# Mixer of a two-block network: three tiles on the unnormed input, gate tile later, VectorE's program in another order

## What is computed

```python
hn = rmsnorm(x, norm_mix_g)            # x * rsqrt(mean(x*x) + eps) * g, per token
z = hn @ w_in                          # 1024 -> u,v | a,g | xc | oc | 4+4 gates
# head group A: u * (causal W_s @ standardize(v) + b_s)        "gating"
# group B: 31-tap causal depthwise conv of a*sigmoid(g), group norm, silu   "long convolution"
# group C: 4-tap causal conv + silu of xc ("short convolution"), then 4 mLSTM heads:
#   logi, logf = gates; running sum and running max over the tokens ("rows"); q, k, v;
#   scores * exp(weights); standardize; skip; sigmoid(oc)
h = x + concat([y_a, y_b, y_c]) @ w_out
# then cross attention on mem, a gated MLP and the whole second block
```

## Time and profile before

| what | value |
|---|---|
| median of 3 runs | 1892.98 us (1892.58 to 1893.07) |
| the profiled execution's own time | 1892.58 us |
| its span in the trace | 1890.8 us |
| PE busy with matmuls | 1866.1 us, 99% of the span |
| POOL / DVE / ACT busy | 1078.7 / 780.8 / 429.9 us |
| share of PE in the chain that ended last | 96% |

### The profile page before, as it was taken

One profiled execution on the slowest core, in us unless ns is written; L12 is line 12 of the kernel. 1 busy time (PEld: TensorE's weight loads), 2 busy tenths in 40 slices (PEclk: granted clock), 3 DMA queues, 4 the chain that ended last, 5 costly groups with the idle time before them and its releaser, 6 DMA issues.

```text
span 1890.8 us, 24359 instructions
## 1 busy us (share of the span) xinstructions
PE 1866.1 (99%) x8992; PEld 1509.4 (80%) x8992; DVE 780.8 (41%) x1274; ACT 429.9 (23%) x840; POOL 1078.7 (57%) x622
## 2 busy tenths in 40 slices
...
GB/s 227 110 81 95 104 96 38 90 100 96 116 89 112 101 78 144 89 46 1 78 79 96 92 100 89 89 90 89 105 96 45 78 90 102 101 100 96 100 101 45
DMA packets 47456, 173.78 MB, mean 92 GB/s; under 512 B 5265, under 2 KB 5905, under 8 KB 46737
## 3 DMA queue, kind: packets, MB, share of 16 engines
...
## 4 chain that ended last, share of the span: by engine, by line
PE 96%; DVE 2%; ACT 1%; DMA 0%; issue 0%; SPq 0%; DVEq 0%
PE acc L513 17%; PE acc L515 17%; PE acc L514 17%; PE acc L540 6%; PE acc L537 6%; PE acc L536 6%; PE acc L592 1%; PE acc L990 1%; PE acc L594 1%; PE acc L593 1%; PE misc L1006 1%; PE misc L1026 1%; PE acc L1182 1%; PE acc L1184 1%; PE acc L1183 1%; PE acc L613 1%
## 5 line engine op out<-in xcount | busy, mean ns | idle before, releaser
L2623 POOL TENSOR_SCALAR w_hi<-raw 128x1024 fp32r<-128x1024 f32 x309 | 335.1, 1084 | 759.3 <-PE acc L540 280.5
L2625 POOL TENSOR_TENSOR w_lo<-raw,w_hi 128x1024 fp32r<-128x1024 f32 x309 | 748.3, 2422 | 25.8
L513 PE MATMUL acc<-x_hi,w_hi 128*128 128x512 f32 x872 | 340.1, 390 | 0.0
L515 PE MATMUL acc<-x_hi,w_lo 128*128 128x512 f32 x872 | 339.3, 389 | 0.0
L514 PE MATMUL acc<-x_lo,w_hi 128*128 128x512 f32 x872 | 339.3, 389 | 0.0
L1952 DVE TENSOR_TENSOR h<-acc,h 128x512 f32<-128x512 f32 x112 | 77.4, 691 | 361.4 <-PE acc L515 230.6
L513 PE MATMUL acc<-y_hi,w_hi 128*128 128x512 f32 x540 | 211.3, 391 | 0.0
L515 PE MATMUL acc<-y_hi,w_lo 128*128 128x512 f32 x540 | 210.1, 389 | 0.0
L514 PE MATMUL acc<-y_lo,w_hi 128*128 128x512 f32 x540 | 210.1, 389 | 0.0
L515 PEld LDWEIGHTS acc<-x_hi,w_lo 128*128 128x128 f32 x872 | 163.7, 188 | 34.2
L513 PEld LDWEIGHTS acc<-x_hi,w_hi 128*128 128x128 f32 x872 | 163.7, 188 | 34.0 <-issue 0.3
...
## 6 DMA issues: line engine op xcount, KB each, us to landing
raw<-weights_dram SPq DMA_DIRECT2D x309, 512.0 KB, 3.5
...
```

Source lines behind the costliest of these rows:

```text
L513: mm(out, m["w_hi"][:, slot, k], hi[:, k], start=k == 0, stop=False)
L515: last = mm(out, m["w_lo"][:, slot, k], hi[:, k], start=False, stop=k == kc - 1)
L2623: nc.gpsimd.tensor_scalar(hi, m["raw"][:, slot], 1.0, 0.0, ALU.mult, ALU.add).then_inc(sem("weights_high"), 1)
L2625: nc.gpsimd.tensor_tensor(m["w_lo"][:, slot].rearrange("p k n -> p (k n)"), m["raw"][:, slot], bf(hi), ALU.subtract).then_inc(sem("weights ...
```

## The change

In `weight_stream` the gates' tile goes from place 0 to place 8, and the others ahead of it move up by one: tiles 0 to 3 are now xc, 4 and 5 the sigmoid gates, 6 and 7 a, 8 the gates. ACT first makes x * g and its high part (`y_hi`), DVE the low part (`y_lo`), and PE multiplies tiles 0, 1 and 2 with these (`unnormed`); ACT squares x only afterwards, the sum over features stands inside tile 2, and DVE multiplies the three finished banks by 1/root (`r_late`, in `unnormed_out`) between the steps of the norm. `pair_opening` now serves tiles 3, 4 and 5. SP loads weights tile 0 and the parameters `par` ahead of x, x in four parts, and the constants after weights tile 1; POOL splits tile 0 in two halves. PE runs four matmuls on `sum_h` at the start in place of the idle products. The tokens tiles 13, 14 come ahead of the turns of the gate rows, and `cell_in(0)` waits for 16 tiles out, not 17. `conv_mean` moves behind `cell_out(0)`, `gating` into head 1 behind `cell_scores(1)`. On DVE the rows and masks stay ahead of the long convolution, but both products into `b_in` come ahead of the rows; statistics of v, `cell_diagonal(0)` and the centring of v come between and right behind the taps, the rest of v's norm behind `cell_norm(0)`, with 8 steps for 12. Three small products for later norms move behind the stage `mix_out`.

```diff
@@ -145,8 +145,10 @@
 
     gates = np.zeros((D, P), np.float32)
     gates[:, 0:4], gates[:, 32:36] = w_in[:, 2048:2052], w_in[:, 2052:2056]
+    for c in [8, 9, 10, 11, 6, 7, 4, 5]:
+        add(w_in, chunk(c))
     add(gates, slice(0, P))
-    for c in [8, 9, 10, 11, 6, 7, 4, 5, 12, 13, 14, 15]:
+    for c in [12, 13, 14, 15]:
         add(w_in, chunk(c))
     add_wide(w_in[:, 256:512], 256)
     for c in (0, 1):
...
+        if name == "mix":
+            return self.misc[:, 2], self.misc[:, 1], [self.misc[:, 3], self.misc[:, 1], self.misc[:, 0]]
...
+    def unnormed(k, slots):
+
+        pe.wait_ge(sem("plain_high"), k + 1)
+        for slot in slots:
+            mm(acc[:, slot], m["w_hi"][:, slot, k], y_hi[:, k], start=k == 0, stop=False)
+            mm(acc[:, slot], m["w_lo"][:, slot, k], y_hi[:, k], start=False, stop=False)
+        pe.wait_ge(sem("plain_low"), k + 1)
+        for slot in slots:
+            last = mm(acc[:, slot], m["w_hi"][:, slot, k], y_lo[:, k], start=False, stop=k == KC - 1)
+            if k == KC - 1:
+                last.then_inc(sem("tile_done"), 1)
+
+    pe.wait_ge(sem("warm"), 1)
+    for _ in range(4):
+        mm(acc[:, 3], m["sum_h"][:, 0:P], m["sum_h"], start=True, stop=True)
+    pe.wait_ge(sem("first_half"), 1)
+    for k in range(HALF):
+        unnormed(k, (0,))
+    claim(0)
+    claim(1)
+    for k in range(HALF):
+        unnormed(k, (1,))
+    for k in range(HALF, KC):
+        unnormed(k, (0, 1))
+    claim(2)
+    for k in range(KC):
+        if k == 3:
+            pe.wait_ge(sem("const_in"), 16)
+            sum_squares("mix")
+        unnormed(k, (2,))
+
     def memory_norm(k):
         if k == 6:
             pe.wait_ge(sem("norm_rstd"), 1)
             sum_squares("mem", MEM)
 
-    pair_opening(0, x_hi, x_lo, "norm_high", "norm_ready", 0, 4, 0, memory_norm)
-    stage("mix_in", x_hi, x_lo, 10, at=3)
+    pair_opening(3, x_hi, x_lo, "norm_high", "norm_ready", 0, 3, 2, memory_norm)
+    stage("mix_in", x_hi, x_lo, 7, at=6)
+    tokens(13, 256, x_hi, x_lo, TB)
     pe.wait_ge(sem("xconv"), 4)
     pe.wait_ge(sem("rows"), 2)
     for sb in range(TB):
@@ -673,7 +709,6 @@
     for sb in range(TB):
         last = turn(misc[:, 0, 16 + 4 * sb:20 + 4 * sb], m["row_em"][0:4, blk(sb)], ident[0:4, 0:4])
     last.then_inc(sem("row_cols"), 1)
-    tokens(13, 256, x_hi, x_lo, TB)
...
     def conv_mean(c):
-        pe.wait_ge(sem("conv_b"), c + 1)
-        mm(misc[:, 2 + c], pr.view("avg64"), m["conv_b"][:, c], start=True, stop=True).then_inc(sem("std_mean"), 1)
+        pe.wait_ge(sem("tap%d" % c), CONV_B)
+        mm(misc[:, c], pr.view("avg64"), m["conv_b"][:, c], start=True, stop=True).then_inc(sem("std_mean"), 1)
...
-        pe.wait_ge(sem("std_centred"), c + 1)
+        pe.wait_ge(sem("cell_norm"), 1)
...
+            pe.wait_ge(sem("std_centred"), 2)
...
+            pe.wait_ge(sem("y_a"), 2)
         else:
-            pe.wait_ge(sem("y_a"), 2)
+            for c in range(2):
+                pe.wait_ge(sem("tap%d" % c), CONV_B)
...
-    pe.wait_ge(sem("tile_out"), START["mem_kv"])
+    pe.wait_ge(sem("tile_out"), START["mem_kv"] - 1)
     pe.wait_ge(sem("row_cols_out"), 2)
     cell_in(0)
-    for c in range(2):
-        conv_mean(c)
     pe.wait_ge(sem("norm_ready"), chunks_before("mem") + KC)
     mem_k(0)
     cell_scores(0)
-    for c in range(2):
-        gating(c)
     mem_k(1)
     cell_out(0)
+    for c in range(2):
+        conv_mean(c)
     mem_v(0)
     for head in range(1, 4):
         cell_in(head)
         mem_k(2 * head)
         cell_scores(head)
+        if head == 1:
+            for c in range(2):
+                gating(c)
         mem_k(2 * head + 1)
...
+    act.wait_ge(sem("par_in"), 16)
     for k in range(KC):
-        act.wait_ge(sem("x_in%d" % (k // HALF)), 16)
+        act.wait_ge(sem("x_in%d" % (k // 2)), 16)
+        if k >= 2:
+            act.wait_ge(sem("plain_low"), k - 1)
+        own.link(f(pr.late_bank(k), m["h"][:, k], ACT.Copy, scale=pr.col("norm_mix_g", k)))
+        f(m["y_hi"][:, k], pr.late_bank(k), ACT.Copy).then_inc(sem("plain_high"), 1)
+    for k in range(KC):
         square("mix", k, m["h"])
-    rms_rstd("mix")
+    rstd, summed, _ = pr.norm_banks("mix")
+    act.wait_ge(sem("norm_summed"), 1)
+    rsqrt(m["r_late"], summed, 1.0 / D, RMS_EPS, "r_mix")
+    act.wait_ge(sem("r_mix"), 1)
+    f(rstd, m["r_late"], ACT.Copy).then_inc(sem("norm_rstd"), 1)
...
-    rms_high("mem", m["mn_hi"], MEM, range(4))
-    act.wait_ge(sem("par_in"), 16)
-    act.wait_ge(sem("tile_done"), 1)
+    act.wait_ge(sem("tile_done"), 3)
+    rms_high("mem", m["mn_hi"], MEM)
+    act.wait_ge(sem("tile_out"), 3)
+    out(3, 3, m["xc"][:, 3, CONV_C - 1:])
+    for c in range(2):
+        out(4 + c, c, z[:, 2 + c], ACT.Sigmoid)
+    for c in range(4):
+        act.wait_ge(sem("xconv_pre"), c + 1)
+        f(m["xconv"][:, c], misc[:, c, :], ACT.Silu).then_inc(sem("xconv"), 1)
+    act.wait_ge(sem("tile_done"), 9)
+    act.wait_ge(sem("tile_out"), 8)
     own.mark(f(z[0:4, 0], acc[0:4, 0], ACT.Identity, bias=pr.col("b_igate", 0, 4)))
     fr, rt = z[0:4, 1], m["row_t"][0:4]
-    out(0, 0, fr, ACT.Identity, src=acc[32:36, 0], bias=pr.col("b_fgate", 0, 4))
-    for c in range(2):
-        out(1 + c, (1 + c) % RING, m["xc"][:, c, CONV_C - 1:])
-    rms_high("mem", m["mn_hi"], MEM, range(4, KC))
-    act.wait_ge(sem("tile_out"), 1)
+    out(8, 0, fr, ACT.Identity, src=acc[32:36, 0], bias=pr.col("b_fgate", 0, 4))
+    act.wait_ge(sem("tile_out"), 9)
     own.link(f(rt, fr, ACT.Abs))
     own.link(f(rt, rt, ACT.Exp, scale=-1.0))
     f(rt, rt, ACT.Ln, bias=1.0).then_inc(sem("row_ln"), 1)
-    out(3, 3, m["xc"][:, 2, CONV_C - 1:])
-    out(4, 0, m["xc"][:, 3, CONV_C - 1:])
-    for c in range(2):
-        out(5 + c, (5 + c) % RING, z[:, 2 + c], ACT.Sigmoid)
-    for c in range(4):
-        act.wait_ge(sem("xconv_pre"), c + 1)
-        f(m["xconv"][:, c], misc[:, c, :], ACT.Silu).then_inc(sem("xconv"), 1)
-    act.wait_ge(sem("tile_out"), 9)
...
+    v.memset(m["sum_h"], 1.0).then_inc(sem("warm"), 1)
+    for k in range(KC):
+        dve.wait_ge(sem("plain_high"), k + 1)
+        v.tensor_tensor(m["y_lo"][:, k], pr.late_bank(k), bf(m["y_hi"][:, k]), ALU.subtract).then_inc(sem("plain_low"), 1)
...
+    def unnormed_out(k):
+        if k in (0, 1, 3):
+            t = (0, 1, None, 2)[k]
+            dve.wait_ge(sem("tile_out"), t)
+            dve.wait_ge(sem("tile_done"), t + 1)
+            v.tensor_tensor(m["xc"][:, t, CONV_C - 1:], acc[:, t], m["r_late"], ALU.mult).then_inc(sem("tile_out"), 1)
+
+    dve.wait_ge(sem("r_mix"), 1)
+    rms("mix", h, "norm_mix_g", m["x_hi"], m["x_lo"], also=unnormed_out)
...
-        dve.wait_ge(sem("tile_out"), 3 + 2 * pair)
+        dve.wait_ge(sem("tile_out"), (2, 4)[pair])
...
+    for c in range(2):
+        dve.wait_ge(sem("tile_out"), 6 + c)
+        dve.wait_ge(sem("tile_done"), 7 + c)
+        v.tensor_tensor(m["b_in"][:, c, CONV_B - 1:], acc[:, 2 + c], z[:, 2 + c], ALU.mult)\
+            .then_inc(sem("tile_out"), 1)
...
+    def rows():
+
+        dve.wait_ge(sem("row_ln"), 1)
+        own.link(v.scalar_tensor_tensor(fr, fr, 0.0, row("row_t"), ALU.min, ALU.subtract))
+        v.tensor_tensor_scan(row("row_F"), fr, fr, 0.0, ALU.add, ALU.min).then_inc(sem("rows"), 1)
...
+    def long_taps(first, end):
+
+        for j in range(first, end):
+            for c in range(2):
+                if j:
+                    dve.wait_ge(sem("tap%d" % c), j)
+                conv_step(misc[:, 2 + c, :] if j < CONV_B - 1 else m["conv_b"][:, c], m["b_in"][:, c, j:j + S],
+                          pr.col("conv_b_w", 2 * j + c), pr.col("conv_b_b", c) if j == 0 else None, misc[:, 2 + c, :])\
+                    .then_inc(sem("tap%d" % c), 1)
...
+    def values_centred():
+
+        own.settle()
+        dve.wait_ge(sem("v_a_stats"), 1)
+        for tb in range(TB):
+            own.mark(v.scalar_tensor_tensor(vt[:, tb], vt[:, tb], mv[:, tb, 0:1], pr.view("ln_a_g"),
+                                            ALU.subtract, ALU.mult))
+
+    def values_normed():
+
+        own.settle()
+        dve.wait_ge(sem("v_a_rstd"), 1)
+        for tb in range(TB):
+            last = v.scalar_tensor_tensor(vt[:, tb], vt[:, tb], m["v_rstd"][:, tb:tb + 1], pr.view("ln_a_b"),
+                                          ALU.mult, ALU.add)
+            if tb < TB - 1:
+                own.mark(last)
+        last.then_inc(sem("v_a_ready"), 1)
+
...
+        if head == 0:
+            conv_centred()
...
+    rows()
+    dve.wait_ge(sem("tile_out"), 8)
+    dve.wait_ge(sem("xconv"), 4)
+    long_taps(0, 27)
+    value_stats()
+    long_taps(27, 29)
     cell_diagonal(0)
-    dve.wait_ge(sem("tile_out"), START["mem_kv"])
-    gate(0)
+    own.link(v.memset(m["v_c"][:, :, P:], 1.0))
+    long_taps(29, CONV_B)
+    values_centred()
     cell_weights(0)
-    gate(1)
     cell_norm(0)
+    values_normed()
     for head in range(1, 4):
```

(57 more changed lines are left out.)

82 lines of the change are left out of this document (35 added, 47 removed).

## The result

| | before | after |
|---|---|---|
| median | 1892.91 us (1892.58 to 1893.07, 4 runs) | 1905.76 us (1903.44 to 1906.14, 4 runs) |
| profiled execution, span | 1892.58, 1890.8 us | 1905.44, 1903.7 us |

The ratio is 1.0063, 95% interval 1.0051 to 1.0075: 0.6% slower. The forecast was 1895.0 us with a range to 1898.2, so it was 10.8 us too low, and the measured time lies outside the range.

A forecast was written before the change was run, and what follows sets the result against it. PE, busy 99% of the span, was taken to bound the kernel. Work moved, balanced against the new wait, gave -0.5 us and the clock +2.6, so +2.1 on the median 1892.98: 1895.0 us, range 1890.8 to 1898.2.

The forecast's parts named there:

- The opening: Start of the kernel to tile 5: x*g starts at 6.4, gaining 5.2 us, plus 0.69 if the first head doesn't wait.
- the waits that I summed: PE in the opening: 1.4 us lost before tiles 3 and 4, 0.8 more at the sum for mem.
- The gate chain: ACT's gate rows: 5.9 us, 2.6 of it two table loads without drain; DVE, idle since 61.9, gets rows at 68.85.
- Rows and masks 9.0: DVE ahead of the taps: rows and masks, 2.9 + 6.06 and a handoff, take 9.0 us.
- I take 1.4, since 256 columns is half: Centring of v on DVE, four steps on 256 columns: between 1.3 and 2.6 us, taken as 1.4.
- The wait at `cell_out(0)`: Head 0: PE arrives at 119.65, DVE's operands at 125.0, so PE waits 5.35 us.
- In head 1 itself I find no further wait: Head 1 on PE: v's norm ends 1.4 us after `cell_norm(0)`, when PE has just finished the scores; no wait.
- the edits at nothing: Three edits counted as nothing: second-norm products behind `mix_out`, halved split of tile 0, v's norm in 8 steps for 12.
- The clock: PE's clock falls inside the wait at `cell_out(0)`, costing 2.6 us; bounds 0 and 2.6.
- rival: Four: clock holds (0.15), opening starves PE further (0.19), no wait at `cell_out(0)` (0.10), table loads with drain (0.04).

The follow-up runs named there:

- e2: The change with the first 24 taps of the long convolution on DVE ahead of the row operations instead of behind them; 1896.18 us, ratio 1.0013.
- e12: The change with v's norm reading its second tensor from a PSUM bank, gain and bias left out; 1899.25 us, ratio 1.0029.
- e5: The change with both groups of v's norm moved on DVE into its wait for `cell_out(0)`; 1896.37 us, ratio 1.0019.
- e7: The change with the edits of e2 and e5 together; 1890.22 us, ratio 0.9987 to the kernel before.
- e9: e7 with the last four operations of v's norm behind the subtraction of the convolution's mean; 1889.34 us, ratio 0.9979.
- e3: The change with v's norm reading one tensor, a column of numbers replacing gain and bias; 1904.13 us, ratio 1.0055.
- e4: The change with ACT's small logarithm, which draws its table in, moved ahead of the copies of tile 9; 1902.30 us, ratio 1.0050.
- e1: The change plus unread products on PE, five ahead of `cell_out(0)` and two ahead of the gating in head 1; 1899.78 us, ratio 1.0035.
- e11: e9 with the two halves of the gating, and the DVE products that use them, in heads 1 and 2; 1888.78 us, ratio 0.9974.

## Why the prediction was wrong

The forecast of 2.1 us more than before puts the turn of head 0 at 148.23 + 2.1 = 150.3; it came at 160.97, 10.7 later. By step:

- **The opening, mis-sized.** x*g began at 7.66, not 6.4: the count of bytes gave the place in the queue, but x landed 1.3 later. `cell_in(0)` came at 109.3 in place of 107.8. Forecast gain 5.9, measured 4.4. Of the waits that I summed, 1.4 and 0.8, the trace has 1.26 and 0.6.
- **The gate chain, right.** Both loads, no drain behind them, DVE idle 7.0 us and rows at 70.41, which is 68.85 and the opening's 1.5.
- **"Rows and masks 9.0", mis-sized.** They took 10.7. Scans and row products read SBUF and were stretched beside splits: `row_F` took 3.30 here and 1.21 in e2, `row_em` 2.70 here and 0.68 in e2. The windows of the earlier trace rows held such stretches too (`row_M` 3.30 of the 6.06), in other places, and I took them for fixed.
- **"I take 1.4, since 256 columns is half", mis-sized.** The taps have a tensor in PSUM and are not held up; the centring is, 2.80. e12 shows what it takes when free, 1.65.
- **The wait at `cell_out(0)`, right in place and cause**, 6.9 for 5.35. With the above `cell_out(0)` began at 129.47 and not 125.0: 4.5 us. The wait grew by less, since PE came there 2.9 later than I summed: 1.5 for the opening and 1.2 for the wait at `mem_k(1)`, which I did not have.
- **"In head 1 itself I find no further wait": the step that failed.** I gave v's norm 1.4 us behind `cell_norm(0)` and called it hidden. It took 4.53, PE waited 2.1, and the clock fell a second time. The free operations take 1.65 (e12), so 1.4 was near for a norm that nothing holds up; what was missing is that POOL's splits hold it up. I had also listed v's norm among the edits at nothing, without the price if it is not hidden: that price was 2.1 and 4.6 us.
- **The clock, right once.** It fell in the first wait, at 126.3 us, and cost 1.8, in `cell_out(0)` alone, where I took 2.6. That a wait of 2 us could be followed by 10 us at half rate was in no rival.

Sum: 4.5 - 0.8 + 2.1 + 4.6 = 10.4 of the 10.7. Shown by runs: the waits' price (e2, e5, e7, e9); the cause of the long norm (e5 and e12); that the second stretch belongs in its long form to the wait (e2, e3 and e4 keep both; e5, e7 and e12 have neither; e1 waits 0.4 us there and stays at full rate). Not shown is why the clock falls behind some short waits and not behind others. The opening itself was sound: it is worth 4 us, which e11 has and the change spent.
